# The query projection as seven Strassen products in a hybrid convolution and attention block

## The reference

```python
h = rmsnorm(x, attn_norm_g)                     # 512 x 1024
proj = h @ w_in                                 # columns: conv B | conv C | conv x | q | k | v | gate_conv | gate_attn
y_conv = (u_b * short_conv(u_c * u_x, conv_w)) @ w_conv_out
attn = sliding_window_attention(q, k, v, sinks, rel_bias)   # 16 heads of 64, 2 k/v heads
y_attn = attn @ w_attn_out
mixed = sigmoid(g_conv) * y_conv + sigmoid(g_attn) * y_attn
x = x + mixed @ w_o
h2 = rmsnorm(x, mlp_norm_g)
x = x + square(relu(h2 @ w_up)) @ w_down        # 1024 -> 4096 -> 1024
out = rmsnorm(x, final_norm_g)
```

## Time and profile before

| | us |
|---|---|
| median of 3 runs | 757.71 (757.3 to 758.04) |
| the profiled execution | 757.86, of which the span is 756.1 |
| TensorE busy | 745.3 (99%) |
| VectorE busy | 646.3 (85%) |
| ScalarE busy | 419.8 (56%) |
| TensorE's granted clock, mean | 0.997 of full speed |

### The profile page before, as it was taken

How to read it: one execution, slowest core, us unless ns; L and a number is a source line. 1 busy time by engine, 2 the same in 40 slices (tenths; PEclk the granted TensorE clock), 3 DMA queues, 4 the chain that set the end, 5 groups by cost and what they waited for, 6 DMA issues and landing times.

```text
span 756.1 us, 10473 instructions
## 1 busy us (share of the span) xinstructions
PE 745.3 (99%) x4067; PEld 646.6 (86%) x4067; DVE 646.3 (85%) x748; ACT 419.8 (56%) x535; POOL 81.9 (11%) x117
## 2 busy tenths in 40 slices
PE   8999999999999999999999999999999999999996
PEld 7888888888888888888878899889988999899985
DVE  5766688889899686989899999998799879986997
ACT  7424555453644656664548776654465355545555
POOL 3202000121112101001000101010101010000102
PEclk9999999999999999999999999999999999999998
DMA  7727513143237996766965746767677767676703
GB/s 256 248 83 279 168 55 112 57 108 114 72 123 223 293 263 169 222 166 187 301 180 138 222 142 168 211 178 193 190 175 190 200 168 207 183 198 191 196 1 112
DMA packets 69408, 131.22 MB, mean 174 GB/s; under 512 B 2604, under 2 KB 22132, under 8 KB 69364
## 3 DMA queue, kind: packets, MB, share of 16 engines
q1 hardware_dynamic: 50400, 84.18, 33.4%
q0 software_dynamic: 18752, 46.15, 27.6%
q10 hardware_dynamic: 212, 0.28, 0.1%
HBM read 124.29 MB, written 6.32 MB: 173 GB/s over the span
## 4 chain that ended last, share of the span: by engine, by line
PE 90%; DVE 4%; DMA 3%; issue 2%; ACT 1%; SPq 0%; DVEq 0%; ACTq 0%
PE pair L959 38%; PE pair L918 21%; PE pair L727 8%; PE pair L729 8%; PE pair L728 8%; DMA home_raw<-in_w_attn_out 2%; PE pair L774 2%; DVE home_lo L1756 1%; PE pair L749 1%; PE pair L748 1%; PE pair L758 1%; DMA xn<-in_x 1%; PE pair L820 1%; DVE mixed L1948 0%; DVE s_lo_tile L1812 0%
## 5 line engine op out<-in xcount | busy, mean ns | idle before, releaser
L1191 ACT ACTIVATE high<-home_raw 128x2048 fp32r<-128x2048 f32 x91 | 174.3, 1915 | 147.3 <-PE pair L959 96.7
L1756 DVE TENSOR_TENSOR home_lo<-home_raw,high 128x2048 fp32r<-128x2048 f32 x91 | 208.4, 2290 | 37.2 <-ACT high L1191 36.8
L959 PE MATMUL pair<-high,s_hi_tile 128*128 128x512 f32 x440 | 110.3, 391 | 0.0
L959 PE MATMUL pair<-high,s_lo_tile 128*128 128x512 f32 x440 | 110.0, 390 | 0.1
L959 PE MATMUL pair<-home_lo,s_hi_tile 128*128 128x512 f32 x440 | 109.3, 389 | 0.0
L727 PE MATMUL pair<-h,wgt 128*128 128x512 f32 x256 | 101.5, 397 | 0.0
L729 PE MATMUL pair<-h,wgt 128*128 128x512 f32 x256 | 99.9, 390 | 0.0
L728 PE MATMUL pair<-h,wgt 128*128 128x512 f32 x256 | 99.8, 390 | 0.0
L959 PEld LDWEIGHTS pair<-high,s_lo_tile 128*128 128x128 f32 x440 | 82.4, 188 | 17.6 <-DVE s_lo_tile L1812 0.5
L959 PEld LDWEIGHTS pair<-home_lo,s_hi_tile 128*128 128x128 f32 x440 | 82.5, 188 | 17.1
L959 PEld LDWEIGHTS pair<-high,s_hi_tile 128*128 128x128 f32 x440 | 81.8, 188 | 17.2 <-ACT pair L1283 0.5
(11 more groups left out here) (215 smaller groups left out, 1001.8 us busy)
## 6 DMA issues: line engine op xcount, KB each, us to landing
raw<-in_w_in SPq DMA_DIRECT2D x34, 512.0 KB, 4.6
home_raw<-in_w_up SPq DMA_DIRECT2D x16, 1024.0 KB, 5.5
home_raw<-in_w_down SPq DMA_DIRECT2D x16, 1024.0 KB, 5.1
home_raw<-in_w_up POOLq DMA_DIRECT2D x12, 1024.0 KB, 8.3
home_raw<-in_w_down POOLq DMA_DIRECT2D x12, 1024.0 KB, 8.3
home_raw<-in_w_in POOLq DMA_DIRECT2D x7, 1024.0 KB, 8.3
home_raw<-in_w_in SPq DMA_DIRECT2D x7, 1024.0 KB, 6.5
home_raw<-in_w_conv_out SPq DMA_DIRECT2D x4, 1024.0 KB, 5.1
```

Of the source, the lines that this page charges most:

```text
L959: last = mm(pair[region(s, i)][:, b, :], a_[:, k, b * P:(b + 1) * P], w[:, k, :], start=(fresh and kind == 0 and k == 0), stop=(kind == 2 ...
L1191: a(high[n % 2][:, :], home_raw[home_of(s, name)][:, :], ACT.Copy).then_inc(m_hi, 1)
L1756: v.tensor_tensor(home_lo[home][:, :], home_raw[home][:, :], f32(high[n % 2][:, :]), ALU.subtract).then_inc(m_lo, 1)
```

## The change

The q projection becomes one Strassen stage of its own. A product is 4 weight tiles x 4 channel tiles x 3 kinds = 48 matmuls 256 wide; seven of them make 336. Products M1 and N2 need only the first 256 tokens. They run before the k/v strip, and the transposes of the last 256 tokens stand inside N2. Then come k/v, M6, M5, M7, M3 and N4.

- x blocks 0 and 1 are loaded first, then M1's weights in two halves, x blocks 2 and 3, N2's two halves, the base of T3, and the k/v weights. The last block is scaled like the others, without the diagonal.
- The tiles of the late tokens are copied twice by ScalarE, once split into `h` and once whole into `qa`; VectorE takes the sums of h from there, with one addition less in each of the first two sums.
- The sums of h, T2, and the low parts of M6, M5 and M7 follow the late tiles on VectorE. T3, T1 and T4 of q are completed by adding DMAs from GpSimd (`add_q`).
- Results are gathered in `qa` by copies of ScalarE (`q_copy`) and additions of VectorE (`q_add`).
- Loads of the mixer strips are written out instead of in a loop, and wait for q products.
- In AO, `s4` moves ahead of the low part of M6 on VectorE, and SP's first load for WO waits until T1 has been completed (`t1_in`) where it waited for T1's base (`t1_base`).

```diff
--- before.py
+++ after.py
+        Q_REGION = {N2: 0, M5: 2, M3: 2}
...
+            load_x(0)
+            load_x(1)
+            load_q_half(M1, 0, 0, q_b11[0])
+            load_q_half(M1, 0, 1, q_b11[1])
+            load_x(2)
+            load_x(3)
+            load_q_half(N2, 1, 0, q_b21[0])
+            load_q_half(N2, 1, 1, q_b21[1])
+            load_q(M7, 0, 1, q_t3_base)
             load_t(S_KV, 0, 0, w_in, COL_KV)
-            load_t(S_Q, 0, 0, w_in, COL_Q)
-            for i in range(1, 3):
-                load_t(S_Q + i, 0, 0, w_in, COL_Q + SC * i)
+            sp.wait_ge(xt_ready, 8)
+            load_q(M5, 0, 0, q_t1_base)
+            sp.wait_ge(lo_ready, 2)
+            load_q(M3, 1, 1, q_b22)
             sp.wait_ge(ext_step, 1 + BUCKETS)
             sp.dma_start(bias_rows[:, :], ext[:, :]).then_inc(bias_out, 16)
             sp.wait_ge(bias_out, 16)
-            sp.wait_ge(xt_ready, KT)
+            sp.wait_ge(q_prod, 6)
+            load_t(S_MIX, 3, 0, w_in, COL_C)
+            sp.wait_ge(q_prod, 8)
             band = bass.AP(bias_rows, 0, [[1, P], [3 * P, HEADS], [1, 2 * P]])
             sp.dma_start(bias[:, :, :], band).then_inc(bias_in, 16)
-            load_t(S_Q + 3, 0, 0, w_in, COL_Q + SC * 3)
-            with sp.Fori(0, 4) as n:
-                it = Pass(n, 0, 4)
-                load_t(S_MIX, 3, it, w_in, n * SC + COL_C)
-                load_t(S_MIX + 1, 3, it, w_in, n * SC + COL_X)
-                load_t(S_MIX + 2, 3, it, w_in, n * SC + COL_B)
+            sp.wait_ge(q_prod, 12)
+            for n in range(4):
+                if n:
+                    load_t(S_MIX, 3, n, w_in, n * SC + COL_C)
+                load_t(S_MIX + 1, 3, n, w_in, n * SC + COL_X)
+                load_t(S_MIX + 2, 3, n, w_in, n * SC + COL_B)
...
-            sp.wait_ge(t1_base, 16 * (AO + 1))
+            sp.wait_ge(t1_in, 16 * (AO + 1))
...
+            def add_q(i, kh, nh, done):
+                pool.dma_start(q_raw[i][:, :].rearrange("p (k n) -> p k n", k=4),
+                               w_in.rearrange("(k p) n -> p k n", p=P)[:, cols(4 * kh, 4), cols(COL_Q + 512 * nh, 512)],
+                               accum_op=ALU.add).then_inc(done, 16)
             g.memset(ext[:, :], NEG).then_inc(ext_step, 1)
+            pool.wait_ge(q_t3_base, 16)
+            add_q(M7, 1, 1, q_t3_in)
...
+            pool.wait_ge(q_t1_base, 16)
+            add_q(M5, 0, 1, q_t1_in)
...
+            store_sum(M6)
+            pool.wait_ge(q_low, 5)
+            add_q(N4, 1, 0, q_t4_in)
+            store_sum(M5)
+            store_sum(M7)
+            store_sum(M3)
...
+            x_transposes(1)
+            idle_transposes(4)
+            def q_product(i, between={}):
...
+                for kind in range(3):
+                    w, a_ = ((whi, ahi), (whi, alo), (wlo, ahi))[kind]
+                    early_ = i in (M1, N2)
+                    if early_:
+                        order = [(k, f) for e in range(2) for k in (2 * e, 2 * e + 1) for f in range(4)] if kind < 2 else \
+                            [(k, f) for f in range(4) for k in range(4)]
+                    else:
+                        order = [(k, f) for f in range(4) for k in range(4)]
+                        if kind == 0:
+                            pe.wait_ge(q_high, at_ + 3)
+                        elif kind == 2:
+                            pe.wait_ge(q_low, at_ + 3)
+                        if i in HS:
+                            if kind < 2:
+                                pe.wait_ge((hs_split, hs_ready)[kind], H_SUMS[i] + 1)
+                    seen = 0
+                    for k, f in order:
+                        if early_ and k + 1 > seen:
+                            seen = k + 1
+                            if kind == 0:
+                                pe.wait_ge(h_hi, 4 * at_ + k + 1)
+                                if k % 2 == 0:
+                                    pe.wait_ge(q_high, 2 * at_ + k // 2 + 1)
+                            elif kind == 1:
+                                pe.wait_ge(h_ready, 4 * at_ + k + 1)
+                            elif k % 2 == 0:
+                                pe.wait_ge(q_low, 2 * at_ + k // 2 + 1)
+                        last = mm(acc[:, f, :], w[:, k, f * P:(f + 1) * P], a_[:, k, :],
+                                  start=(i in (M1, N2, M5) and kind == 0 and k == 0 and f % 2 == 0),
+                                  stop=(kind == 2 and k == 3), skip_group_check=True)
+                        if kind == 2 and k == 3 and f % 2 == 1:
+                            last.then_inc(q_prod, 1)
+                    if kind in between:
+                        between[kind]()
+            def late_transposes():
+                pe.wait_ge(h_ready, 8)
+                x_transposes(2)
+                x_transposes(3)
+            def kv_strip():
                 w = wgt[weight_slot(S_KV)][:, :, :].rearrange("p c (k n) -> p c k n", k=KT)
-                for k, j in [(k, j) for k in range(4) for j in range(2)] + [(k, j) for j in range(2) for k in range(4, KT)]:
-                    if j == 0 and k == 0:
-                        pe.wait_ge(first_lo, 1)
-                    elif j == 0 and k in (2, 4):
-                        pe.wait_ge(lo_ready, k // 2)
-                    pe.wait_ge(h_ready, max(k, j) + 1)
-                    half = cols((1 - j) * P, P)
-                    wh, wl = w[:, 0, k, half], w[:, 1, k, half]
-                    mm(bank[j][:, :], wh, h[:, 0, k, :], start=(k == 0), stop=False)
-                    mm(bank[j][:, :], wh, h[:, 1, k, :], start=False, stop=False)
-                    last = mm(bank[j][:, :], wl, h[:, 0, k, :], start=False, stop=(k == KT - 1))
-                    if k == KT - 1:
-                        last.then_inc(half_ready[j], 1)
-            first_strip()
+                for j in range(2):
+                    for at_, k in enumerate(LATE_TILES):
+                        if j == 0:
+                            pe.wait_ge(lo_ready, k // 4 + 1)
+                            pe.wait_ge(h_ready, 8 + max(at_, 2) + 1)
+                        half = cols((1 - j) * P, P)
+                        wh, wl = w[:, 0, k, half], w[:, 1, k, half]
+                        first, end = at_ == 0, at_ == KT - 1
+                        acc = bank[B_KV + j][:, :]
+                        mm(acc, wh, h[:, 0, k, :], start=first, stop=False)
+                        mm(acc, wh, h[:, 1, k, :], start=False, stop=False)
+                        last = mm(acc, wl, h[:, 0, k, :], start=False, stop=end)
+                    last.then_inc(half_ready[j], 1)
+            q_product(M1)
+            q_product(N2, {1: late_transposes})
+            kv_strip()
+            pe.wait_ge(q_c11_base, 1)
...
-            with pe.Fori(0, 2) as i:
-                it = Pass(i, 0, 2)
-                transposed_strip(S_Q, 2, it, 1, 2, h)
-                transposed_strip(S_Q + 1, 2, it, 2, 2, h)
+            q_product(M6)
+            q_product(M5)
+            pe.wait_ge(q_c12_base, 1)
+            q_product(M7)
             value_transposes()
+            pe.wait_ge(q_c22_base, 1)
+            q_product(M3)
+            pe.wait_ge(q_c22, 1)
+            q_product(N4)
+            pe.wait_ge(q_c11, 1)
...
+            def tile_high(half, at_, k):
+                act.wait_ge(xt_ready, 4 * half + k % 4 + 1)
+                gain_ = pcol[:, g1 + k:g1 + k + 1]
+                t = cols(2 * P * half, 2 * P)
+                a(h[:, 0, k, t], tile_of(k), ACT.Copy, scale=gain_).then_inc(h_hi if not half else wide, 1)
+                if half:
+                    a(qa[:, k, t], tile_of(k), ACT.Copy, scale=gain_).then_inc(h_hi, 1)
+            root(0)
+            root(1)
+            q_high_half(M1, 0)
+            q_high_half(M1, 1)
             act.wait_ge(par_ready, 1)
-            for k in range(KT):
-                if k == 2:
-                    first_weights(1)
-                if k == KT // 2:
-                    hi_chunks(S_KV, chunks=(1,))
-                act.wait_ge(xt_ready, k + 1)
-                a(h[:, 0, k, :], bank[k][:, :], ACT.Copy, scale=pcol[:, g1 + k:g1 + k + 1]).then_inc(h_hi, 1)
-            hi_chunks(S_Q)
+            for k in range(4):
+                tile_high(0, k, k)
+            root(2)
+            for k in range(4, 8):
+                act.wait_ge(h_ready, k - 3)
+                tile_high(0, k, k)
+            q_high_half(N2, 0)
+            q_high_half(N2, 1)
+            root(3)
+            hi_chunks(S_KV)
+            for at_, k in enumerate(LATE_TILES):
+                if k // 4:
+                    act.wait_ge(h_ready, 8 + LATE_TILES.index(k - 4) + 1)
+                tile_high(1, at_, k)
...
+            q_copy(0, 0, M1, q_c11_base)
+            sum_high(M6)
+            q_high_part(M6)
             act.wait_ge(half_ready[0], 1)
...
+            sum_high(M5)
+            q_high_part(M5)
+            q_copy(0, 1, M6, q_c12_base, -1.0)
+            sum_high(M7)
```

(68 more changed lines are left out.)

234 lines of the change are left out of this document (125 added, 109 removed).

## The result

The kernel became slower: a median of 762.70 us (762.38 to 762.98, 4 runs) against 757.66 (757.30 to 758.04), a ratio of 1.0066 with a 95% interval of 1.0049 to 1.0084. The forecast was 755.0. The profiled execution has a span of 760.9 us in place of 756.1, at a mean granted clock of 0.994.

The account below looks back on a forecast made before the run. TensorE, busy for 99% of the span, was taken as the bound. From the profiled 757.86 us, -2.7 in the q stage plus 0 at the attention output gave 755.15, as a median 755.0; range 753.2 to 757.6.

Parts of the forecast that it names:

- The q stage: Front of the kernel: M1 starts earlier and TensorE has less work, so the mixer starts at 65.75 against 68.48, -2.7 us.
- Rival 3: Front: the clock falls in TensorE's 1.2 us gap ahead of M1, giving 760.8 to 764.6 us; chance 0.06.
- The attention output: SP's wait and the s4 move there turn TensorE's 1.57 us of waits into 0 to 3.9; term taken as 0.
- Beside two plain loads I expect as much: Attention output: T3 of the output projection takes 10.7 us as before and lands at 376.4.
- VectorE's 3.2 us: Attention output: VectorE comes about 3.2 us earlier to the output projection's sum T2, at 373.6 instead of 376.77.
- s4 moved: Attention output: s4 put into VectorE's hole, one of two edits whose joint term was taken as 0.
- Rival 2: Late transfers: T3 near 379 adds 2.3 us, or the q stage's T1 1.6; 756.6 to 757.3 us; chance 0.21.

Follow-up runs that it names:

- experiment 1: The changed kernel with SP's first load for WO waiting for T1's base again, not for the finished T1: 757.08 us, ratio 0.9994.
- experiment 2: The kernel before with only SP's wait changed from T1's base to the finished T1: 763.34 us, ratio 1.0075.
- experiment 5: The changed kernel with SP's loads of WO's B21 and the residual held until T3 has landed: 759.44 us.
- experiment 6: The changed kernel with T1's base of WO, on GpSimd's own queue, held until T3 has landed: 762.52 us.
- experiment 9: The changed kernel with VectorE's sums T2 and T4 of WO moved behind the merges, transfers unaltered: 758.02 us, ratio 1.0007.
- experiment 13: The kernel of experiment 7 with VectorE's sum T4 of WO alone moved behind the last merge: 755.24 us, ratio 0.9972.
- experiment 3: The kernel before with only s4 of AO moved ahead of the low part of M6 on VectorE: 757.49 us, ratio 1.0001.
- experiment 4: The kernel of experiment 1 with GpSimd's addition for T3 of WO held until T1 of AO has landed: 759.71 us, ratio 1.0037.
- experiment 7: The changed kernel without SP's wait for the finished T1, WO's B12 loaded early, T3's addition held until T1 landed: 756.84 us, ratio 0.9992.

## Why the prediction was wrong

- **The q stage: right, 0.8 us too hopeful.** -2.7 was the sum and -1.94 came. M1 started at 11.01 (10.9), the k/v strip at 25.29 (24.7), M6 at 36.70 (36.2), the mixer at 66.54 (65.8). The waits were 0.77, 0.28 and 0.31 where 0.4, 0.6 and 0.4 stood, M7 had none, and the products kept their 0.120 us a matmul (32 in 11.01 to 14.94, 0.123). Most of the 0.8 us was there before M6: 0.6 at the strip, of which 0.37 is its wait.
- **Rival 3: refuted.** The clock was 1.00 from 0 to 30 us; the gap of 1.34 us ahead of M1 cost nothing but itself. The last three numbers are clock, DMA share and GB/s:

```profile
10.00:12.00 2.00, 0.99 (x8) 0.99 (x9) 1.55 (x4) 2.00 (x6) 0.00 (x0) 1.00 1.01 400
```

- **The attention output: the failed step.** "Beside two plain loads I expect as much", 10.7 us for T3, landing at 376.4, with 13.4 as the upper bound. It took 16.4 and landed at 381.4. (The forecast's 376.4 is on the time of the kernel before; with TensorE's lead of 2 us it would be 374.4.) The bound was the longest addition of the kernel before, at 254.08 us, which had one load of SP issued 2.5 us ahead of it and one 2.9 us behind it. The row for T3 itself was read without its neighbours: before, B11 and B21 left at 366.12, when T3 had been under way for 8 of its 10.7 us. Holding T1 alone on the engines moved T3's start from 358.07 to 364.98, just behind the moment at which B11 and B21 leave. The term was 0, between -1.6 and +2.3; it was +6.8: 6.3 of waiting, 1.26 of low clock, less 0.76 between the merges. Experiments 1 and 2 show that this one edit makes it, 5 and 6 that SP's loads stretch T3 and the transfer of its own queue does not, and 9 that VectorE's order turns its late landing into idle time of TensorE; the low clock, 0.50 and 0.71 in the windows, adds the 1.26.
- **VectorE's 3.2 us: mostly not there.** It was ready for T2's sum at 373.83 in place of 376.77, 2.9 us earlier, of which 2.05 are TensorE's lead. T1's base took 8.69 us where 7.38 stood before, so T1 landed later than the sum had it. This cost nothing here, since T3 came later still.
- **A second miss, hidden by the first.** Even without that edit the forecast's 755 was not to be had (757.08). The prediction carried the front's gain straight to the end. But the transfers of the attention output follow one another (T1's base, its addition, T3), and they were already the last to arrive: the earlier trace rows has ScalarE idle 5.20 us for T1 and TensorE waiting 1.57 us behind it. With TensorE 1.3 us earlier M5 waits too. Only experiment 13, with transfers and sums both out of the way, keeps the whole of it. Its 755.24 beside the forecast's 755.0 is luck, as it has three edits that the forecast knew nothing of.
- **s4 moved: nothing**, as taken (experiment 3).
- Rival 2 named the right kind of thing, a late T3, and priced it at 2.3 us, because it took the bound from other neighbourhoods. It also left out the clock, though 6 us without matmuls had 0.67 in the earlier trace rows.

What stays open: why the base of the attention output's T1 takes 8.6 to 9.2 us in every trace with the new q stage and 7.4 to 7.5 in every one without it, beside the same load. The difference is as much as the 1.16 us that M5 waits in experiment 1. All but its last packets were through in time: in 350 to 352 us the DMA share was 0.08 in experiment 1 and 0.62 before. Open too are why T3 had no packet in its first 5 us, how B21 and the residual share the blame, and what the last 0.88 us at 398 would need.

## What to carry to other kernels

A gain at the front of a kernel is worth only what the next place that was bound by transfers lets through; look for waits there that are already above nought before adding it to the sum. When a wait is added so that one transfer runs alone, ask what it pushes the next transfer into, and price that by the loads issued in the same microseconds, not by the range seen elsewhere. Of two transfers that leave together the later one can pay for both, so read which one was late before moving either (experiments 4 and 7). And an in-order engine that waits for a transfer nobody needs yet can often be cured by moving that one instruction behind the urgent ones, if the new place has slack.

## What the runs showed of the hardware

- With additions the DMA engines are as full as with plain loads and move half the bytes. In the kernel before, 360 to 364 us holds two additions and nothing else, 344 to 348 us of the changed kernel two plain loads; the last two columns are share and GB/s.

```profile
360.00:364.00 4.00, 4.00 (x19) 3.30 (x18) 3.25 (x3) 0.33 (x1) 0.00 (x0) 1.00 1.13 208
```

```profile
344.00:348.00 4.00, 4.00 (x19) 3.30 (x19) 4.00 (x4) 0.48 (x2) 0.00 (x0) 1.00 1.04 405
```

- One addition of 1 MB took 8.2 to 8.8 us with little beside it, 9.5 when it left 3.5 us ahead of SP's B21 (experiment 7), 10.9 when it left 1.7 us ahead of it (experiment 4), and 15.3 to 16.4 when it left with SP's two loads or just behind them; a second transfer behind it on GpSimd's queue made 0.65 us. B21 itself took 14.4 us in experiment 7, 16.4 in experiment 4 and 10.0 in the changed kernel.
- The clock did not follow the length of the idle alone. It fell around waits of 2.43, 4.90 and 6.17 us (eight matmuls in 3.41, 3.78 and 3.44 us), and held at 1.00 in every window from 376 to 392 us around one of 3.23 us in experiment 5, where the eight took 2.11:

```profile
383.99 2.11 PE L1075 MATMUL pair<-high,s_hi_tile 128*128 128x512 f32 x8 [3.23 <-DVE zc L2102]
```
